# Second block of a two-block model: reordered units, shorter pooled-mean and Fourier matmuls

## The reference

```python
def _fourier_branch(u, z, w_fourier):
    uf = u.astype(jnp.float32).reshape(b, n, F_HEADS, F_DIM)
    y = jnp.fft.fftn(uf, axes=(1, 3), norm='ortho').real.reshape(b, n, W_F)
    return jax.nn.silu(z) * (y @ w_fourier)

def _pool_branch(u, z, pool_w, pool_scale):      # windows 2, 4, 8, 16
    mean = (cs[:, hi, sl] - cs[:, lo, sl]) / (hi - lo)
    d = mean - u[..., sl]
    outs.append(d @ pool_w[i])
    return jax.nn.silu(z) * (jnp.concatenate(outs, -1) * pool_scale)

out = jnp.concatenate([o_f, o_att, o_c, o_p], axis=-1) @ w_out
x_new = x + gate[:, None] * out
```

## Time and profile before

| | |
|---|---|
| time, median of 3 runs | 1391.8 us (1391.75 to 1392.01) |
| time of the profiled execution | 1391.53 us |
| its span, first to last instruction | 1389.7 us |
| mean granted TensorE clock | 0.999 |
| TensorE matmuls busy | 97% of the span |
| TensorE weight loads busy | 88% |
| VectorE / ScalarE / GpSimd busy | 62% / 53% / 9% |
| DMA | 269.54 MB, mean 194 GB/s |

### The profile page before, as it was taken

How to read it: one execution, slowest core, us unless ns; L and a number is a source line. 1 busy time by engine, 2 the same in 40 slices (tenths; PEclk the granted TensorE clock), 3 DMA queues, 4 the chain that set the end, 5 groups by cost and what they waited for, 6 DMA issues and landing times.

```text
span 1389.7 us, 24840 instructions
## 1 busy us (share of the span) xinstructions
PE 1348.2 (97%) x10420; PEld 1225.6 (88%) x10420; DVE 868.1 (62%) x1295; ACT 739.9 (53%) x1200; POOL 122.1 (9%) x72
## 2 busy tenths in 40 slices
PE   6999999999999999999999999999999999998998
PEld 2898998998999998998899989999997778687978
DVE  3557976667779876579665476444574536428754
ACT  3466476564745534565656646454554464326552
POOL 0000000200000000000000110000103432142000
PEclk9999999999999999999999999999999999999999
DMA  9955555677699995644743558875551212032420
GB/s 345 377 187 182 171 202 195 199 272 234 224 337 367 356 362 181 211 139 163 240 152 122 194 180 293 299 250 175 174 170 61 92 61 91 31 100 92 152 91 31
DMA packets 194722, 269.54 MB, mean 194 GB/s; under 512 B 5037, under 2 KB 174386, under 8 KB 188338
## 3 DMA queue, kind: packets, MB, share of 16 engines
q1 hardware_dynamic: 194610, 267.94, 57.0%
HBM read 266.87 MB, written 1.05 MB: 193 GB/s over the span
## 4 chain that ended last, share of the span: by engine, by line
PE 80%; DVE 10%; ACT 4%; issue 2%; DMA 1%; SPq 1%; DVEq 0%; ACTq 0%
PE first_dense L1671 14%; PE first_dense L1675 13%; PE first_dense L1673 13%; PE first_dense L1007 5%; PE first_dense L1010 5%; PE first_dense L1009 5%; DVE first_w_lo L544 2%; PE first_s L1671 2%; PE first_s L1675 2%; PE first_s L1673 2%; PE first_misc L240 2%; PE first_dense L1844 2%; ACT first_w_hi L538 1%; PE first_o L1675 1%; PE first_o L1673 1%
## 5 line engine op out<-in xcount | busy, mean ns | idle before, releaser
L544 DVE TENSOR_TENSOR first_w_lo<-first_raw,first_w_hi 128x1024 fp32r<-128x1024 f32 (+2 forms) x304 | 367.0, 1218 | 229.2 <-ACT first_w_hi L538 227.3
L538 ACT ACTIVATE first_w_hi<-first_raw 128x1024 fp32r<-128x1024 f32 (+2 forms) x304 | 313.8, 1041 | 239.3 <-PE first_dense L1675 92.9
L1671 PE MATMUL first_dense<-first_h_parts,first_w_hi 128*128 128x256 f32 x1312 | 374.6, 285 | 2.2 <-DVE first_h_parts L2299 1.7
L1673 PE MATMUL first_dense<-first_h_parts,first_w_hi 128*128 128x256 f32 x1312 | 371.2, 283 | 0.0
L1675 PE MATMUL first_dense<-first_h_parts,first_w_lo 128*128 128x256 f32 x1312 | 371.1, 283 | 0.0
L1671 PEld LDWEIGHTS first_dense<-first_h_parts,first_w_hi 128*128 128x128 f32 x1312 | 251.5, 192 | 12.4 <-issue 9.2
L1673 PEld LDWEIGHTS first_dense<-first_h_parts,first_w_hi 128*128 128x128 f32 x1312 | 251.6, 192 | 0.1
L1675 PEld LDWEIGHTS first_dense<-first_h_parts,first_w_lo 128*128 128x128 f32 x1312 | 251.6, 192 | 0.0
L1009 PE MATMUL first_dense<-first_parts,first_w_hi 128*128 128x512 f32 (+1 forms) x400 | 137.0, 343 | 0.0
L1007 PE MATMUL first_dense<-first_h_parts,first_w_hi 128*128 128x512 f32 (+1 forms) x336 | 118.1, 352 | 0.9 <-DVE first_w_lo L694 0.9
L1010 PE MATMUL first_dense<-first_h_parts,first_w_lo 128*128 128x512 f32 (+1 forms) x336 | 115.6, 344 | 0.0
(11 more groups left out here) (407 smaller groups left out, 2640.4 us busy)
## 6 DMA issues: line engine op xcount, KB each, us to landing
first_raw<-in_w_in SPq DMA_DIRECT2D x78, 1024.0 KB, 5.3
first_raw<-in_w_ff SPq DMA_DIRECT2D x64, 1024.0 KB, 6.8
first_units<-in_w_ada SPq DMA_DIRECT2D x34, 1024.0 KB, 6.2
first_units<-in_w_mod SPq DMA_DIRECT2D x17, 1024.0 KB, 6.7
first_raw<-in_w_out SPq DMA_DIRECT2D x16, 1024.0 KB, 4.9
first_mb<-in_w_ada SPq DMA_DIRECT2D x10, 1024.0 KB, 8.0
first_mb<-in_w_mod SPq DMA_DIRECT2D x7, 1024.0 KB, 7.6
first_raw<-in_w_uq SPq DMA_DIRECT2D x6, 768.0 KB, 4.5
```

Source lines behind the costliest of these rows:

```text
L538: act.activation(w_hi[g % SPLIT][:, c], raw[g % CHUNK_RING][:, c], ACT.Copy).then_inc(hi_made, 1)
L544: dve.tensor_tensor(w_lo[g % SPLIT][:, c], raw[g % CHUNK_RING][:, c], w_hi[g % SPLIT][:, c].bitcast(F32), ALU.subtract).then_inc(lo_made, 1)
L1671: pe.matmul(out, still[0](t), moving[0](t), start=start and t == n == 0, stop=False, skip_group_check=True)
L1673: pe.matmul(out, still[0](t), moving[1](t), start=False, stop=False, skip_group_check=True)
```

## The change

The order of `todo` changes in both layers. Before, layer 0 had `ch zc zp zf up uf pool_mean`, four `fourier_head`, `pool_out fourier_seq fourier_out out`, two units of each. After it has `ch zc up uf pool_mean zp`, head 0, `zf` 0, heads 1 to 3, `zf` 1, `fourier_seq pool_out fourier_out out`. Layer 1 had the same order as layer 0 with two heads; after it has `ch zc up uf pool_mean zp`, heads 0 and 1, `zf fourier_seq pool_out fourier_out out`. The attention of layer 1 starts its jobs ahead of units 6, 8, 9, 11 instead of 6, 8, 10, 12. The convolution follows `up` (layer 0) or the head and the pooled mean (layer 1).

`pool_mean` multiplies only the output columns that a half of the positions reaches (`pool_reach`), and goes through the two halves outside of the two column groups. `fourier_seq` computes the cosine sum for positions 0 to 128 and the sine sum for 1 to 127, and the evacuation builds all 256 from their sum and difference: two copies on ScalarE, then an add and a subtraction on VectorE. The rest of the diff merges seven semaphores of the kernel's start into one, `opening_turned`, with fixed values for each of its users.

```diff
@@ -860,10 +864,14 @@
             kv = [("k", 0), ("v", 0)]
             todo = of("q") + (kv + of("cb") + of("cc") + of("za") if ctx_out else of("za") + kv + of("cb") + of("cc"))
-            for name in ("ch", "zc", "zp", "zf", "up", "uf", "pool_mean"):
+            for name in ("ch", "zc", "up", "uf"):
                 todo += of(name)
-            todo += [("fourier_head", t) for t in range(T // P)]
-            for name in ("pool_out", "fourier_seq", "fourier_out"):
+            heads = [("fourier_head", t) for t in range(T // P)]
+            if ctx_out:
+                todo += of("pool_mean") + of("zp") + heads[0:1] + [("zf", 0)] + heads[1:4] + [("zf", 1)]
+            else:
+                todo += of("pool_mean") + of("zp") + heads + of("zf")
+            for name in ("fourier_seq", "pool_out", "fourier_out"):
                 todo += of(name)
@@ -888,9 +896,16 @@
+            def two_parts(bank):
+                return bank[:].rearrange("p (a t) -> p a t", a=2)
+
+            def spectrum(e):
+                return yf[:, e, :].rearrange("p (s t) -> p s t", s=2) if ctx_out else yf[:, :, 0:S]
-            job_step, job_lag = ([9 + 2 * n for n in range(8)], 2) if ctx_out else ([6, 8, 10, 12], 1)
+            job_step, job_lag = ([9 + 2 * n for n in range(8)], 2) if ctx_out else ([6, 8, 9, 11], 1)
@@ -935,8 +950,8 @@
-            conv_step = {unit_no["up" if ctx_out else "pool_out", e]: e for e in range(PARTS)}
-            conv_begin = {} if ctx_out else {unit_no["fourier_head", T // P - 1]: 0}
+            conv_step = {unit_no["up", e] if ctx_out else unit_no["fourier_head", e]: e for e in range(PARTS)}
+            conv_begin = {} if ctx_out else {unit_no["pool_mean", 0]: 0}
@@ -1130,13 +1145,13 @@
-                                for g in (2 * (e * NH + i), 2 * (e * NH + i) + 1):
-                                    r = HD * (g % 2)
-                                    for tt in range(TT):
-                                        last = pe.matmul(by_half(bank)[r:r + HD, i, s * S:(s + 1) * S],
-                                                         up2[:, 2 * s + tt, g * HD:(g + 1) * HD],
-                                                         k2[:, K2_POOL + (4 * tt + g) * S:K2_POOL + (4 * tt + g + 1) * S],
-                                                         start=tt == 0, stop=tt == TT - 1)
+                                for tt in range(TT):
+                                    for g in (2 * (e * NH + i), 2 * (e * NH + i) + 1):
+                                        r, (lo, hi) = HD * (g % 2), pool_reach(tt, g)
+                                        at = K2_POOL + (4 * tt + g) * S
+                                        last = pe.matmul(by_half(bank)[r:r + HD, i, s * S + lo:s * S + hi],
+                                                         up2[:, 2 * s + tt, g * HD:(g + 1) * HD], k2[:, at + lo:at + hi],
+                                                         start=tt == 0, stop=tt == TT - 1, skip_group_check=True)
@@ -1156,12 +1171,12 @@
-                                    for part in range(2):
+                                    for part, (to, lo, hi) in enumerate(((0, 0, N_EVEN), (N_EVEN, 1, S - N_EVEN + 1))):
                                         at = K2_FN + (2 * tt + part) * S
-                                        last = pe.matmul(by_half(bank)[:, i, s * S:(s + 1) * S],
+                                        last = pe.matmul(by_half(bank)[:, i, s * S + to:s * S + to + hi - lo],
                                                          ab[:, 2 * s + tt, e * NH + i, part * P:(part + 1) * P],
-                                                         k2[:, at:at + S], start=tt == 0 and part == 0,
-                                                         stop=tt == 1 and part == 1)
+                                                         k2[:, at + lo:at + hi], start=tt == 0 and part == 0,
+                                                         stop=tt == 1, skip_group_check=True)
@@ -1282,8 +1297,14 @@
+                    elif name == "fourier_seq":
+                        y, sums = spectrum(e), two_parts(bank)
+                        act.activation(y[:, :, S - 1:N_EVEN - 1:-1], sums[:, :, N_EVEN:S], ACT.Copy)
+                        act.activation(y[:, :, 0:N_EVEN:N_EVEN - 1], sums[:, :, 0:N_EVEN:N_EVEN - 1], ACT.Copy).then_inc(
+                            odd_moved.sem, 1)
@@ -1530,6 +1551,14 @@
+                    elif name == "fourier_seq":
+                        y, sums = spectrum(e), two_parts(bank)
+                        reach(dve, odd_moved, e + 1)
+                        link(dve.tensor_tensor(y[:, :, 1:N_EVEN - 1], sums[:, :, 1:N_EVEN - 1],
+                                               y[:, :, S - 1:N_EVEN - 1:-1], ALU.add))
+                        dve.tensor_tensor(y[:, :, N_EVEN:S], sums[:, :, N_EVEN - 2:0:-1], y[:, :, N_EVEN:S],
+                                          ALU.subtract).then_inc(done.sem, 1)
@@ -2620,6 +2649,7 @@
+N_EVEN = S // 2 + 1
@@ -2651,6 +2681,13 @@
+def pool_reach(tt, g):
+    left = POOL_WINDOWS[g] // 2
+    right = POOL_WINDOWS[g] - 1 - left
+    return (0, P + left) if tt == 0 else (P - right, S)
```

More of the change, by code:

```diff
@@ L1933, in tensor @@
                         pe.transpose(t_bank[0][:, 0:n_rows2], rows2, k[0:n_rows2, K_IDENT:K_IDENT + n_rows2]).then_inc(
-                            cols2_turned, 1)
+                            opening_turned, 1)
                     if l == DEPTH - 1:
@@ L2478, in _ @@
                 n = 3 * KT
-                pe.transpose(c_ps, c_rows, k[0:n, K_IDENT:K_IDENT + n]).then_inc(c_turned, 1)
+                pe.transpose(c_ps, c_rows, k[0:n, K_IDENT:K_IDENT + n]).then_inc(opening_turned, 1)
                 pe.wait_ge(pos_ready, 1)
-                pe.matmul(pos_ps, k[0:1, K_ONES:K_ONES + P], pos_f, start=True, stop=True).then_inc(pos_spread, 1)
+                pe.matmul(pos_ps, k[0:1, K_ONES:K_ONES + P], pos_f, start=True, stop=True).then_inc(opening_turned, 1)
                 def start_unit(i):
@@ L2500, in _ @@
                     if t % 2:
-                        last.then_inc(x_turned, 1)
+                        last.then_inc(opening_turned, 1)
                 start_unit(4)
@@ L2506, in _ @@
                                         k[0:N_ROWS, K_IDENT:K_IDENT + N_ROWS])
-                last.then_inc(cols_turned, 1)
+                last.then_inc(opening_turned, 1)
                 for t in range(KT):
```

28 lines of the change are left out of this document (15 added, 13 removed).

## The result

| | before | after |
|---|---|---|
| median of the timed runs | 1391.9 us (1391.75 to 1392.18, 6 runs) | 1397.3 us (1396.1 to 1400.7, 6 runs) |
| ratio after to before | | 1.0043, 95% interval 1.003 to 1.0055 |
| profiled execution, span | 1391.5 us, 1389.7 us | 1398.7 us, 1396.9 us |
| mean granted clock | 0.999 | 0.993 |
| first `values` of the second block to the last transposes of the kernel | 268.3 us | 274.0 us |

The account below looks back on a forecast made before the run. TensorE, busy 97% of the span, was taken as the bound, so only its work or waits matter. Waits +7.3, work -6.9 and clock +3.0 gave +3.4 us, 1395.2 us (0.24% slower, chance 0.49), range 1388.0 to 1399.8.

Parts of the forecast that it names:

- Column counts, -6.9 us: Shorter `pool_mean` and `fourier_seq` units remove TensorE work: 2.25 us and 4.6 us over three units each.
- The far bound: `fourier_seq` records held by a 190 ns weight load that doesn't shrink: 3.04 us a unit, saving only 1.6 us in all.
- The new evacuation: `fourier_seq`'s evacuation on ScalarE and VectorE takes 1.6 us, 1.0 more than before; bounds 1.3 and 2.4.
- Gate waits: TensorE waits for gate units' banks before `zf` 0, head 2, `fourier_seq` 1 and layer 1's `pool_out`: 1.3, 1.9, 2.3, 2.3 us.
- Attention waits of layer 1: `values` 2 and 3 wait for ScalarE's copies: 1.45 and 2.6 us.
- Waits behind `pool_out`: Layer 0: `pool_out` 1 waits 0.7 us, `fourier_out` 1 and `out` 0 together 0.5; layer 1: `fourier_out` 1.2.
- The convolution, costed at nothing: Convolution steps move in both layers at no cost; without cover, one chain of about 3 us would be exposed.
- Sum without the clock, +0.4 us: Second block's waits +6.7 + 7.6 - 2.0 - 5.0 = +7.3 us, work -6.9; together +0.4.
- The clock, +3.0 us: Two falls to half clock at four new gaps: 1.7 us for one, 1.3 for the pair.
- No further fall: Rival: same waits and work, but the clock stays up; 1392.2 us, chance 0.22.
- The gain is kept: Rival: gate and attention waits lose about half, 14.3 becoming 7.1 us; 1385.0 us, chance 0.15.
- The weight load: Rival: `fourier_seq` bound by weight loads (+3.0 us), reversed operands double VectorE's evacuation part (+1.6); 1399.8 us, chance 0.14.

Follow-up runs that it names:

- e7: The changed kernel with `fourier_seq` evacuated by one ScalarE copy, its addition and subtraction left out (a test, not a version): 1397.8 us, ratio 1.0051.
- e4: The changed kernel with idle f32 matmuls, results unused, on a free bank ahead of six waiting steps: 1393.0 us, ratio 1.0018 to before.
- e1: The kernel before, in its old order, with only the change's halved columns and new evacuation: 1395.9 us, ratio 1.0032.
- e5: As e1, with layer 1's convolution moved ahead (first tile behind `uf`, rest behind the pooled mean): ratio 1.0011 to before, medians' difference +2.2 us.
- e6: Packed version: unit order of before, halved columns, `fourier_seq` ahead of `pool_out`, third bank for the tail, attention and layer 1's convolution earlier: 1389.9 us, ratio 0.9993.
- e9: e6 with layer 1's convolution behind the heads and layer 0's second one behind `uf` 0: ratio 0.9986 to before, medians' difference -1.8 us.
- e12: e11 with the last two attention jobs of layer 0 let go by one unit: 1389.0 us, ratio 0.9986 to before.
- e2: The change's order only, with the full columns and the one-copy evacuation of before: 1398.3 us, ratio 1.0044 to before.
- e3: The changed kernel with a third PSUM bank for some short units, so none waits for a gate unit's bank: 1392.4 us, ratio 1.0001 to before.
- e8: The changed kernel with `zp` and `zf` evacuated by one ScalarE copy, their silu left out (a test, not a version): 1381.5 us, ratio 0.9935.
- e11: Packed version with layer 0's convolution as in e6 and layer 1's as in e9: 1385.1 us, ratio 0.9960 to before.
- e10: e9 with a few filling f32 matmuls into an idle bank ahead of some units: 1388.7 us, ratio 0.9982 to before.

## Why the prediction came out as it did

The sign and the mechanism were right, and the size was 2 us short (3.4 us forecast, 5.4 timed). Step by step:

- **Column counts, -6.9 us**: 0.93 against the 1.02 taken for a pooled mean, 1.94 against 2.05 for `fourier_seq`; three units of each give 2.5 + 4.9 = 7.4. The far bound by the weight load's mean of 190 ns was wrong: that mean is 192 ns in the change as well, at 0.12 us per record. The Trainium skill, "TensorE: Matmul & The Clock Gate", section "LDWEIGHTS (loading the stationary operand)", states a load's time as its columns divided by 1.2 in ns, by which 107 ns is the estimate for 128 columns. The trace shows 192 ns for the duration of a load, so the rule doesn't hold for that; only the pace of 0.12 us per record leaves room for it.
- **The new evacuation**: 1.6 us was forecast, and its parts are 0.36 and 0.17 on ScalarE and twice 0.42 on VectorE, 1.36 us from first to last where nothing stands in its way (1204.62 to 1205.98). The 0.42 that was taken for 254 columns without a row on reversed operands is what the reversed ones took; the same without reversal was not run. e7 shows it free in this order.
- **Gate waits**: forecast 1.3, 1.9, 2.3 in layer 0 and 2.3 in layer 1; measured 1.6, 2.2, 2.5 and 2.5. They are 0.2 to 0.3 longer each: for `zf` of layer 1 the bank is free 4.46 us after the next unit's start (1358.30 to 1362.76) where 4.3 was taken, and `fourier_seq` covers 1.95 of it instead of 2.0. Attention waits of layer 1: 1.45 and 2.6 forecast, 1.4 and 2.9 measured. No `by_keys` wait above 0.6, as forecast.
- **Waits behind `pool_out`** (0.7, 0.5 and 1.2) hardly show in the change, where 0.3 is left. The first and the last were right all the same: TensorE at 1.2 GHz reaches them later, and in e4 they stand at 0.6 and 1.0. The 0.5 shows in neither.
- **The convolution, costed at nothing**: right for the place that the change gives it. But e1, e5, e6 and e9 show that this was the most delicate step of all: the same instructions a unit or more earlier or later made waits of 2 to 5.5 us, and in e12 the attention moved behind them did. The forecast named its price, one chain of 3 us, and not what stands behind it on VectorE.
- **Sum without the clock, +0.4 us**: e4's stretch is 0.36 us longer than before's. So the sum was right, and partly by luck: the work was 0.5 us more than forecast and the waits behind `pool_out` 0.8 less, the gates and the attention 1.2 more. Of e4's timed difference of +2.0, its profiled execution shows another 0.8 ahead of the stretch (1117.85 against 1117.08).
- **The clock, +3.0 us: the term that was mis-judged.** Two falls of the four gaps were taken; all four came. Before's own fall went with the wait of `by_keys`, as forecast; the one behind the last `values` is in its place. The stretch gives 274.0 - 268.6 = 5.4 us for them in the profiled execution, the timed runs 3.4. By the profile this term is 2.4 us short and explains the whole miss; by the medians it is 0.4 short, and 1.6 us of e4's +2.0 stay outside of the sum. So the number of falls was wrong, and how much of the missing 2 us is theirs stays open. The reason given against more falls, a boundary with a wait of 1.9 us at full clock, was one row; the row that bears on it was the 1.9 us gap between short products, which did cost a fall, and all four new gaps (2.2 to 2.9 us) are longer and stand between short products too. That the count could have come out otherwise is shown by e7 and e2, where the gap of 2.2 us cost no fall and that of 1.6 us did.
- **Rivals**: "No further fall" is e4's case; without the filling, the change, e2, e3 and e7 all have more falls in their profiles than before. "The gain is kept" fell with 14.0 us of waits, where it took about 7; e8 shows what it would have been. Its arithmetic was loose: six and not seven of the waits are those of gates and attention, and they sum to 11.9 of the 14.3. The weight load fell with 1.94 us.

What stays open is 1 to 2 us ahead of the stretch. The first `values` start at 1117.08 before, at 1118.50 in the change, and between 1117.03 and 1119.24 in the twelve experiments, with a median near 1117.6. The change merges five semaphores of the kernel's start into one (`c_turned`, `pos_spread`, `x_turned`, `cols_turned`, `cols2_turned`; not seven, as the text on the change has it); e2, which doesn't have that, is the one at 1117.03, but e10, which has it, is at 1117.07. Some executions have a half clock between 14 and 22 us and some don't, and the starts don't follow that. No run undid the merged semaphores alone.

## What to carry to other kernels

A unit whose evacuation goes to and fro between engines (a silu: 4.3 us here) needs a unit of that length behind it, not a short one; a third bank doesn't replace it, since the queues of ScalarE and VectorE hold TensorE by the data instead (e3); count the time from its last matmul to the next user of its bank before shortening or reordering what lies between. When an evacuation moves to another engine, read what already stands in that engine's queue at that place: two instructions of 0.42 us kept TensorE waiting 4.7 (e1). And where TensorE must wait between short products, a few matmuls on a free bank gave 3.4 of 5.4 us back (e4); they gave nothing that can be measured in e10, where the longest gap was left unfilled. Last, read what GpSimd does at the place to which VectorE's work is moved: e12 is slower than e11 mostly by that, as far as durations tell; the next section has them.

## What was not expected of the hardware

- Halving the columns of a plain f32 record halved its time all the way to 0.12 us, with its weight load's duration unchanged at 192 ns in the group's row. The loads overlap (sixteen of 192 ns each in the 1.94 us of a unit), and the mean duration of one is no bound on their rate.
- One VectorE scaling of 128x256 took 2.6 us instead of 0.42 when GpSimd had begun an instruction of the low split just before it. In e9 the three scalings take 3.35 us, and all of the surplus is in the first (timeline of layer 0):

```profile
1186.77 5.11 POOL L697 TENSOR_TENSOR first_w_lo<-first_raw,first_w_hi 128x1024 fp32r<-128x1024 f32 x2 [10.64 <-ACT first_w_hi L690]
...
1189.61 2.55 DVE L1613 SCALAR_TENSOR_TENSOR keep_x<-keep_x,keep_cols,first_small 128x256 f32<-128x256 f32 x1
```

In e6 the last of the same three ends as GpSimd begins (timeline of layer 0):

```profile
1185.01 1.27 DVE L1613 SCALAR_TENSOR_TENSOR keep_x<-keep_x,keep_cols,first_small 128x256 f32<-128x256 f32 x3
...
1186.26 2.39 POOL L697 TENSOR_TENSOR first_w_lo<-first_raw,first_w_hi 128x1024 fp32r<-128x1024 f32 x1 [11.85 <-ACT first_w_hi L690]
```

The scaling of e9 ends at 1192.16, 0.3 us behind the end of GpSimd's second instruction (1191.88), and the next two take 0.4 each. e11 is as e6 (1.27 us for three). In e12 GpSimd's two instructions run from 1182.93 and from 1185.29; two scalings, from 1183.01 and from 1185.53, take 2.60 and 2.56 us, and the other five 0.4 to 0.5 each. The kernel before has one of 2.59 us too. So in e12 some 4.3 of the 5.4 us that `values` waits, and in e9 some 2.1 of the 5.5, are this and not the length of the convolution. That is worked out from the durations; no run moved GpSimd's work away with all else kept.
